# Moving gate tiles and top-k rounds in a hybrid attention kernel

## The reference

```python
z = h @ w_in                                  # all projections, gates g among them
score = where(causal, einsum(w_idx, relu(q_idx @ k_idx.T)), -inf)
_, idx = lax.top_k(score, 256)                # DSA keys, per query
y_a = conv(...); y_d = dsa(...); y_f = fox(...); y_s = swa(...)
gates = sigmoid(g)                            # (L, 4, 1024)
out = sum_n(gates[n] * (y_n @ w_branch[n])) @ w_o
x = x + g1 * rmsnorm(out)                     # then a SwiGLU sub-layer, unchanged here
```

## Time and profile before

| | us |
|---|---|
| median of 3 runs (1734.55 to 1738.4) | 1734.74 |
| the profiled execution | 1735.29 |
| its span, first to last instruction | 1733.5 |
| PE busy in the span | 1680.1 (97%) |
| PE weight loads busy | 1397.3 (81%) |
| DVE busy | 1055.2 (61%) |
| POOL busy | 822.4 (47%) |
| ACT busy | 613.3 (35%) |

### The profile page before, as it was taken

One profiled execution on the slowest core, in us unless ns is written; L12 is line 12 of the kernel. 1 busy time (PEld: TensorE's weight loads), 2 busy tenths in 40 slices (PEclk: granted clock), 3 DMA queues, 4 the chain that ended last, 5 costly groups with the idle time before them and its releaser, 6 DMA issues.

```text
span 1733.5 us, 22877 instructions
## 1 busy us (share of the span) xinstructions
PE 1680.1 (97%) x8072; PEld 1397.3 (81%) x8072; DVE 1055.2 (61%) x1756; ACT 613.3 (35%) x1104; POOL 822.4 (47%) x537
## 2 busy tenths in 40 slices
PE   5999999999999999989999999999999999999997
PEld 4877878787888888879888888888888888888886
DVE  7745745556999999947486445843553454345337
ACT  5544336374222222246423455332223223222323
POOL 2421130102436565620288434675567656655755
PEclk9999999999999999999999999999999999999999
DMA  8131141010111111340575403120112012111205
GB/s 342 37 85 47 51 115 35 16 52 17 61 46 46 45 46 45 112 103 1 217 273 171 170 14 133 37 73 30 66 49 68 29 48 73 48 48 48 73 25 207
DMA packets 37455, 138.87 MB, mean 80 GB/s; under 512 B 4624, under 2 KB 4624, under 8 KB 37392
## 3 DMA queue, kind: packets, MB, share of 16 engines
q1 hardware_dynamic: 35152, 130.70, 21.7%
q0 software_dynamic: 2240, 7.34, 1.9%
HBM read 118.10 MB, written 13.63 MB: 76 GB/s over the span
## 4 chain that ended last, share of the span: by engine, by line
PE 68%; issue 11%; POOL 10%; DVE 4%; DMA 4%; ACT 2%; SPq 1%; POOLq 0%; ACTq 0%; DVEq 0%
PE ps L639 19%; PE ps L640 18%; PE ps L641 18%; POOL w_t L1713 5%; PE ps L863 4%; PE ps L842 2%; PE ps L766 1%; DMA raw<-in_w_ffn 1%; PE ps L767 1%; POOL w_f L1728 1%; DMA region_a<-in_x 1%; PE ps L670 1%; POOL raw L1731 1%; POOL slot_c L1713 1%; DVE region_c L1904 1%
## 5 line engine op out<-in xcount | busy, mean ns | idle before, releaser
L639 PE MATMUL ps<-h_t,w_t 128*128 128x512 f32 x1112 | 437.7, 394 | 3.3 <-DVE h_t L1896 1.6
L641 PE MATMUL ps<-h_t,w_t 128*128 128x512 f32 x1112 | 433.6, 390 | 0.0
L640 PE MATMUL ps<-h_t,w_t 128*128 128x512 f32 x1112 | 433.5, 390 | 0.0
L639 PEld LDWEIGHTS ps<-h_t,w_t 128*128 128x128 f32 x1112 | 209.4, 188 | 49.7 <-issue 5.5
L641 PEld LDWEIGHTS ps<-h_t,w_t 128*128 128x128 f32 x1112 | 209.1, 188 | 44.0
L640 PEld LDWEIGHTS ps<-h_t,w_t 128*128 128x128 f32 x1112 | 209.4, 188 | 42.8 <-issue 0.7
L1564 POOL TENSOR_TENSOR w_t<-raw,w_t 128x1280 fp32r<-128x1280 f32 (+1 forms) x50 | 145.9, 2918 | 198.2 <-ACT w_t L1154 197.9
L2265 DVE TENSOR_TENSOR y_f<-ps,y_f 128x512 f32<-128x512 f32 x120 | 80.7, 686 | 217.5 <-PE ps L641 217.5
L1713 POOL TENSOR_TENSOR w_t<-raw,w_t 128x512 fp32r<-128x512 f32 x80 | 110.2, 1383 | 136.7 <-ACT w_t L1452 136.7
L1950 DVE MAX8 top<-region_b 128x8 f32<-128x384 f32 (+5 forms) x192 | 157.9, 882 | 17.6 <-issue 17.0
L1953 DVE MATCH_REPLACE8 region_b<-top,region_b 128x384 f32<-128x384 f32 (+5 forms) x192 | 166.1, 876 | 0.0
(11 more groups left out here) (286 smaller groups left out, 3345.4 us busy)
## 6 DMA issues: line engine op xcount, KB each, us to landing
raw<-in_w_ffn SPq DMA_DIRECT2D x46, 512.0 KB, 3.9
raw<-in_w_gates SPq DMA_DIRECT2D x32, 640.0 KB, 3.9
region_b<-in_w_ada SPq DMA_DIRECT2D x33, 512.0 KB, 4.5
region_d<-in_w_ffn SPq DMA_DIRECT2D x20, 512.0 KB, 4.0
raw<-in_w_z SPq DMA_DIRECT2D x18, 512.0 KB, 3.4
region_a<-in_x SPq DMA_DIRECT2D x8, 512.0 KB, 14.9
h_f<-in_w_ada SPq DMA_DIRECT2D x8, 512.0 KB, 8.1
raw<-in_w_o SPq DMA_DIRECT2D x8, 512.0 KB, 3.6
```

Of the source, the lines that this page charges most:

```text
L639: pe.matmul(o, a_hi, m_hi, start=first, stop=False, skip_group_check=more)
L640: pe.matmul(o, a_hi, m_lo, start=False, stop=False, skip_group_check=more)
L641: return pe.matmul(o, a_lo, m_hi, start=False, stop=last, skip_group_check=more)
```

## The change

- **Gates beside SWA.** Three halves instead of two run in the tail of the second attention: both of tile 16 and the first of tile 17, in 12 parts (banks 4, 5, 6). The parts are dealt out by `FILL[3]`: 1 and 2 around the values of the last unit but one, 2 and 2 in the last unit, 3 ahead of the last but one `turn_out`, 2 ahead of the last, none after it. For that, tile 17 is split in the middle of the attention (ACT at unit 20, POOL then). After the attention only the other half of tile 17 is left (`gate_second`, bank 7).
- **One gate tile behind the DSA queries.** The order is now 23 gate tiles, the two DSA query tiles (39 and 40), the 24th gate tile (`T_LAST` = 41), DSA attention. Both query tiles use one low-part scratch row, so DVE waits for tile 39's moves ahead of tile 40's low part. Queries go to the other y buffer, D's output to buffer 0. The last mix row is spilled by itself (`s_spill_last`, waited for by ACT at unit 41); the distance table goes to `far` in `region_c`, early.
- **Selection rounds between low parts.** Block 5 (768 columns) gets 13 rounds early: 2 inside the convolution's gating, 2 ahead of the FoX tiles, and 2, 2, 2, 2, 1 between their low parts. The mask operations move behind the low parts of the DSA tiles.
- **Window bias.** It is loaded four units earlier: head 0's 256 columns into a free stretch of the FoX query row (`spare`), the rest into `region_d`.

```diff
+SIDE_BLOCK = 5
+SIDE_ROUNDS = {(0, 1): 2, (1, 0): 2, (2, 0): 2, (2, 1): 2, (3, 0): 1}
+
+FILL = {3: (1, 2, 2, 2, 3, 2), 2: (1, 1, 1, 1, 0, 1), 0: (0,) * 6}
...
-            sp.wait_ge(s_logit, U_SWA)
-            sp.dma_start(region_d[:, :], window_bias).then_inc(s_table, 16)
+            sp.wait_ge(s_logit, U_SWA - 4)
+            sp.dma_start(spare[:, 2 * P:4 * P], window_bias[:, 0:2 * P]).then_inc(s_table, 16)
+            sp.dma_start(region_d[:, 2 * P:L], window_bias[:, 2 * P:L]).then_inc(s_table, 16)
...
+            sp.wait_ge(s_ys, 1)
+            sp.dma_start(far, distance).then_inc(s_table, 16)
+            tile_load(T_LAST, w_gates[3 * KT - 1])
...
+            for dt in range(1, KT - 1):
+                spill(dt, s_spill)
+            tile_load(T_GD, w_gates[3 * KT])
+            spill(KT - 1, s_spill_last)
+            tile_load(T_GD + 1, w_gates[3 * KT + 1])
...
+                fill(parts_at[4])
                 turn_out(end - 2)
                 values(end - 1)
-                next(beside)
+                fill(parts_at[5])
                 turn_out(end - 1)
...
-            attention(U_FOX + 2 * TT, 2 * TT + TT, T_AFS)
+            attention(U_FOX + 2 * TT, 2 * TT + TT, T_AFS, 3)
             pe.wait_ge(s_pt, U_DSA)
             pe.wait_ge(s_of, O_DSA)
+
+            def gate_second(T, buf):
+
+                for _ in gate_half(7, T, 1):
+                    pass
...
                     pe.wait_ge(s_zf, i * 4 + (2 * T + half - 1))
+                    if T == T_LAST:
+                        pe.wait_ge(s_z_lo, lo_halves(T_DSA + 1) + half + 1)
...
-            gate_pairs(T_AFS + 2 * KT, 0)
-            z_group(T_DSA, T_GD - T_DSA)
+            gate_pairs(T_AFS + 2 * KT, 0, KT // 2 - 1)
+            gate_tile(T_DSA - 1, 0)
+            z_group(T_DSA, 2)
+            gate_tile(T_LAST, 0)
             pe.wait_ge(s_moved[T_DSA], 32)
             pe.wait_ge(s_key_in, 64)
...
+                    if gate is not None and u == u0 + 4:
+                        split_hi(gate + 1, n=GT)
...
+                    if u == U_DSA + 1:
+                        act.wait_ge(s_spill_last, 16)
...
+            split_lo(T_DSA)
+            gate_tile(T_DSA - 1, KT - 2, False)
+            split_lo(T_DSA + 1)
+            stack_moves(T_DSA)
+            split_lo(T_LAST)
+            pool.wait_ge(s_key_out, 32)
+            pool.wait_ge(s_spill, 16 * (KT - 2))
+            for i, dst in enumerate((dsa_keys[0][0], dsa_keys[1][0])):
+                for half_rows in rows_of:
+                    pool.dma_start(dst[half_rows], key_dram[:, i, :]).then_inc(s_key_in, 16)
+            stack_moves(T_DSA + 1)
+            split_lo(T_GD)
+            gate_tile(T_LAST, KT - 1, False)
...
-                if T == T_FOX + 1 and half == 0:
-                    dve.wait_ge(s_moved[T_FOX], 32)
+                if T in (T_FOX + 1, T_DSA + 1) and half == 0:
+                    dve.wait_ge(s_moved[T - 1], 32)
...
                 dve.tensor_tensor(pt[c], pt[c], z[:, 2 * c], ALU.mult).then_inc(s_conv, 1)
+                if c == 0:
+                    top_k([SIDE_BLOCK], 2)
...
             forget_spread(0)
+            top_k([SIDE_BLOCK], 2)
             for T in range(T_FOX, T_SWA):
-                stack_lo(T)
-                if T == T_FOX + 1:
-                    forget_sums(0)
+                for half in range(2):
+                    stack_lo_half(T, half)
+                    if T == T_FOX + 1 and half:
+                        forget_sums(0)
+                    elif (T - T_FOX, half) in SIDE_ROUNDS:
+                        top_k([SIDE_BLOCK], SIDE_ROUNDS[T - T_FOX, half])
...
+            while any(n < rounds for n in rounds_done.values()):
+                left = [b for b in rounds_done if rounds_done[b] < rounds]
+                top_k(left, min(rounds - rounds_done[b] for b in left))
+            for T in range(T_DSA, T_LAST):
+                stack_lo(T)
```

More of the change, by code:

```diff
@@ L876, in turn_out, with attention, fill @@
                 mm.then_inc(s_turned, 1)
-            def attention(u0, n, gate=None):
+            def attention(u0, n, gate=None, halves=0):
                 end = u0 + n
-                beside = gate_beside(gate)
+                beside, parts_at = gates_beside(gate, halves), FILL[halves]
+                def fill(parts):
+                    for _ in range(parts):
+                        next(beside, None)
                 logits(u0)
@@ L963, in _ @@
             gate_first(T_AFS, 0)
-            gate_tile(T_AFS + 1, 0)
+            gate_second(T_AFS + 1, 0)
             gate_pairs(T_AFS + 2, 0, KT // 2 - 1)
@@ L995, in column_sums @@
                     mm.then_inc(s_mod, 1)
-            gate_tile(T_WO - 1, 1, read=s_h_read, between=column_sums)
+            gate_tile(T_WO - 1, 0, read=s_h_read, between=column_sums)
             for k in range(KT):
@@ L1294, in exponentials, with attention @@
                                    accum_out=den[:, g % 4, col:col + 1]).then_inc(s_exp, 1)
-            def attention(u0, n):
+            def attention(u0, n, gate=None):
                 end = u0 + n
@@ L1646, in _ @@
             pool.tensor_tensor(y_lo(0), ya_back[:, :, :], y_hi(0).bitcast(F32), ALU.subtract).then_inc(s_ya, 1)
-            gate_pairs(T_AFS, True)
+            gate_tile(T_AFS, 0, True)
+            split_lo(T_AFS + 2, n=GT)
+            gate_tile(T_AFS + 1, 1, True)
+            with order.loop(KT // 2 - 1, 0) as i:
+                for j in range(2):
+                    split_lo(T_AFS + 2 + j + 1, i, 2, GT)
+                    gate_tile(T_AFS + 2 + j, 2 + j, True, i)
             pool.wait_ge(s_ys_hi, 1)
@@ L2122, in _ @@
             attention(U_FOX + 2 * TT, 2 * TT + TT)
-            top_k(range(KB0, TT), rounds - rounds_done[KB0])
-            top_k(range(KB0 + 1, TT), rounds - rounds_done[TT - 1])
-            assert all(n == rounds for n in rounds_done.values())
+            while any(n < rounds for n in rounds_done.values()):
[3 more added lines that the diff above has]
+                stack_lo(T)
             for b in range(KB0, TT):
                 order.mark(dve.tensor_scalar(sc_at[b], sc_at[b], TAKEN / 2, -BIG, ALU.is_gt, ALU.mult))
-            for T in range(T_DSA, T_GD):
-                stack_lo(T)
             order.wait()
-            dve.wait_ge(s_table, 32)
-            dve.wait_ge(s_spill, 16 * (KT - 1))
+            dve.wait_ge(s_table, 48)
+            dve.wait_ge(s_spill, 16 * (KT - 2))
             attention(U_DSA, HEADS * TT)
```

118 lines of the change are left out of this document (61 added, 57 removed).

## The result

| | before | after |
|---|---|---|
| median, us (4 runs each) | 1734.70 (1734.55 to 1738.4) | 1720.68 (1719.94 to 1722.6) |
| span of the profiled execution | 1733.5 | 1720.7 |
| PE busy in the span | 1680.1 | 1674.9 (97%) |
| mean granted clock | 0.992 | 0.995 |

The ratio is 0.9919, 95% interval 0.9905 to 0.9933: 14.0 us faster, where 12.0 were forecast (1720.7 against 1722.7). A second series of the changed kernel gave 1719.61 (0.9917, interval 0.9903 to 0.9930).

The account below looks back on a forecast made before the run. PE's matrix work, busy 97% of the span, was taken to set the time, so only gaps and half clock could be won. 6.3 + 3.4 + 2.8 - 0.5 = 12.0 us faster, 1722.7 us, range 1717 to 1730.

Parts of the forecast that it names:

- What bounds the kernel: Whole kernel: PE busy 97% of the span, so with matmuls unchanged only PE's gaps can be won back.
- A: SWA's tail: gate work covers the 3.47 us gap and its half clock; 6.3 us faster, bounds 5.0 and 6.9.
- B: FoX to SWA: earlier bias load removes a 2.04 us gap and half clock; 3.4 us faster, bounds 5.3 and 1.7.
- C: DSA attention's start: gate tile covers the 5.44 us DMA wait; 2.8 us faster, bounds 5.7 and 1.0.
- The two new waits: PE at tile 41 for tile 40's low part, ACT at unit 41 for the last spill: nothing, 1 us in bound.
- D: Early selection rounds: calls overrun their gaps by 0.3 and 0.8 us; 0.5 us slower, between 0 and 3.
- the text's own test: Whole kernel: the prediction is wrong if the clock dips in a stretch where it did not before.
- DVE in time for tile 39: Ahead of the DSA queries: DVE has 37.6 against 22.7 us, 15 to spare; without side rounds 9 late.
- 1, slow starts: SWA and DSA starts keep ACT waits and extra half clock: 7.5 us less, 1727; chance 0.20.
- 2, the clock stays up: Shorter gaps in B and C bring no half clock: B 5, C 5, A 6.9, D -0.3, 1718; chance 0.10.
- 3: Low parts hold PE at tile 40, or early calls cost the gains: 0 to 4 us less, 1733; chance 0.10.
- 4, POOL and DVE exclude each other at the negation: L2088 held behind tile 17's split and at DSA's start: 15 us, 1738; chance 0.05.

Follow-up runs that it names:

- pool_later: Kernel before with one wait more: POOL's 128x2048 y subtraction waits for DVE's last SWA division; 1729.2 us, ratio 0.9966.
- c_undone: Changed kernel with C alone undone (24 gate tiles, both DSA query tiles, then the attention); 1728.7 us, ratio 0.9957.
- side_only: Kernel before with the 13 side rounds of block 5 alone; 1736.1 us, ratio 1.0008.
- light_side: Changed kernel with 7 side rounds in place of 13, none in the convolution's gating; 1719.6 us, ratio 0.9917.
- neg_pair: Changed kernel with the negation of each maximum written with two SBUF inputs in place of one; 1719.9 us.
- no_side: Changed kernel without any of the 13 side rounds, all of them run late beside the gate tiles; 1729.1 us, ratio 0.9969.

## Why the prediction was right, point by point

**What bounds the kernel**: right. Busy PE fell with the clock losses, and the gain came from gaps and clock alone.

**A**: forecast 6.3, between the traces 6.3, undone 6.3. Each link stands in the rows: the addition is still held (2.81 us where some 4 were said, since it starts later in POOL's subtraction), PE has work over it, and the only gap left is 0.56 where 0.55 was said. pool_later shows the cause that the prediction could only infer from two ends that coincide. It could also have asked what the cheapest cover is: not to start POOL's subtraction early needs one wait.

**B**: forecast 3.4, measured 3.2 between the traces and 3.4 undone. The mechanism was right: the late bias made the gap, and the gap brought the half clock. That the size fits so well is partly luck. It took one wait of 1.74 us off, by the FoX start, and 0.2 for the rest of the chain; there are two waits, 0.40 and 1.25, which come to 1.65 by chance. That they would bring no half clock was assumed, since the FoX row that it used has some.

**C**: forecast 2.8, measured 4.65 (against the 13.91 of c_undone 5.4). The mechanism was right: no wait for a DMA, keys and moves in place. The term that was mis-sized is "the start of any attention", which I took at 10.4 from the FoX start; it is 8.55. That row carried things of its own: a low part on DVE's queue until the first bias (256.43), a table load of 1.28 us on ACT between the first maximum and the first exponential (257.93; at the DSA start it runs while DVE makes the maximum, 756.80), and 3.4 us of half clock. Two rows of before at the FoX start, one of after at the DSA start:

```profile
256.43 1.23 DVE L2085 CUSTOM_DVE_ANT_0 region_a<-ps,region_c 128x1024 f32<-128x1024 f32 x1
257.93 1.28 ACT L1293 ACT_TABLE_LOAD   x1 [2.95 <-DVE neg L2088]
...
756.80 1.28 ACT L1336 ACT_TABLE_LOAD   x1
```

How the 1.86 us between 10.41 and 8.55 divide among the three was not tried. The forecast's bound (no dip, gaps mostly filled, 5.7) named this case, and the sign, 10 to 11 us to the first values, missed it; I put the value at the nearest row without asking what in that row belonged to its place. The two new waits cost nothing, as said: PE had the low part of tile 40 in time, and ACT asked for the last spill at 764.7, 4.3 us after its issue (760.38), without a wait.

**D**: forecast 0.5; between the two traces it looks like 3.6 (3.1 and 0.5), and the text's own test, a clock that dips where it did not before, spoke against it. Two more traces settle it: side_only, +0.2 in the FoX part, and the changed kernel itself, without the stretch at 298. The forecast had put its cost ahead of the FoX logits, and there the five traces without half clock show none beyond their spread of 0.6 us. So 0.5 is a bound rather than a measured price. Where the reasoning was wrong is in adding up overruns: by the issue times of light_side and the other traces, the moves take up most of them.

**DVE in time for tile 39**: forecast 15 us of room, measured 13.4; without side rounds 9 us late was said, and the stage without them was 9.1 longer. The loops did not start when they did before, as I had it, but 3.6 us later (423.23 against 419.61), they got 22.6 us shorter and not 24, and PE came 19.4 us sooner, not 22.7, since the FoX part was long in this execution. Two errors against the forecast and one for it leave 13.4.

**The rivals.** 1, slow starts: false for C and B. 2, the clock stays up: this is what happened in B, C and A, and its C (5) is nearer than mine, but its B (5) and A (6.9) are too high. Its 1718 is 2.7 us off, the forecast 2.0: the measured time lies between the two. 3: no. 4, POOL and DVE exclude each other at the negation: the place was right, the form was not. One input and one column is not held; neg_pair shows that two inputs would be, for 1.24 us, and even then the time stays the same. The Trainium skill, "SBUF — State Buffer", section "Who interferes with whom", says that a DVE instruction with two SBUF inputs contends with a GpSimd instruction that reads SBUF; the trace agrees (0.16 against 1.24 us). For the one-input form the prediction had extended its sentence on two-port modes to a single column, and the two negations that lie beside POOL's work say no, with 154 ns each.

**The sum.** A 6.3, B 3.4, C 4.65 and D -0.2 make 14.15; the medians say 14.0. That these two agree so closely is partly luck: the last series (1734.6 and 1719.6) gives 15.0, and with the 5.4 of c_undone the sum is 14.9. Either way the forecast is 2 to 3 us short, and C, put at 2.8, is where: 1.85 to 2.6 of them.

## What to carry to other kernels

When PE is the bound, look for the places where it idles behind a chain in series (a first logits, maximum, exponential, turn) or behind another engine, and put matmuls over them that have to be done anyway: each such place here cost 3 to 6 us, in SWA's two more than half of it clock, at the FoX start 3.2 even without a loss of clock. Ask first whether one wait, which keeps two engines from excluding each other, does the same. And before a difference of a few microseconds between two traces is explained, look for it in a second trace of the same program.

## What the runs showed of the hardware

- The granted clock and gaps of PE. From the first FoX logits to the end, gaps of 2.0 us and more (2.0 to 2.5 at SWA's start, 3.5 in its tail, 5.4 at the DSA start, 6.8 in no_side) came with half clock every time, 12 of 12, for 6.8 us but once (3.4). It often began before the gap had ended. The SWA and DSA starts with gaps of 0.4 to 1.3 us kept 1.00 every time, 18 of 18. The FoX start, with up to 1.2 and then 1.7 us, was in between: 9 of 11 executions fell to half clock, 7 of them for 3.4 and 2 for 6.8 us. The stretch at 298 followed a gap of 0.69 us, in 2 of these 11 executions.
- The length of a gap alone does not decide. All 13 traces have one of 3.1 us near 36 us, here in before:

```profile
36.32 0.47 PE L639 MATMUL ps<-y_t,h_t 128*128 128x456 f32 x1 [3.12 <-POOL h_t L1571]
```

  In five of them (before, after, no_side, light_side, neg_pair) the clock stays at 1.00 there, in five it falls for 3.4 us and in three for 6.8. So a gap that is found in one trace tells what it may cost, and not what it will.
- DVE and POOL excluded each other for 128x4 and 128x1 operations with two inputs from SBUF (up to 4.13 us where 0.16 is usual) and for a one-input 768-column one (3.7 us), not for a one-input 128x1 one (154 ns, two cases in the trace of after). It goes both ways: POOL's 128x512 addition at 758.22 took 2.13 us beside DVE's 1024-column one, 1.28 alone.
- Moves issued 1.6 us sooner landed no sooner (light_side against after). What paces them was not tried.
